# Three shared accumulator banks for the long convolutions in place of two and one

## The chip, the cores and the metric

The kernel runs on one core of a Trainium2 chip. The metric is the device time of one execution in microseconds (us), as the median of several runs. The core's engines work side by side and meet through semaphores: TensorE (PE in the profile; PEld is its loading of weights), VectorE (DVE), ScalarE (ACT), GpSimd (POOL) and SyncE (SP), which issues most of the DMAs. Matmuls write to accumulator banks; VectorE and ScalarE carry the results out of them into the core's working memory.

## The reference, cut to what matters

The kernel computes one encoder layer with two parallel mixers for a sequence of 1024 tokens and one of 512, width 1024. The part at hand is the gated long convolution, twice in a row over 512 channels:

```python
def hyena_mix(x1, x2, v, kspec, bias):
    def long_conv(z, ks, d):
        zf = jnp.fft.rfft(z, n=2 * L, axis=1)
        return jnp.fft.irfft(zf * ks[None], n=2 * L, axis=1)[:, :L] + d * z
    z = x1 * long_conv(v, kspec[:, 0], bias[0])
    return x2 * long_conv(z, kspec[:, 1], bias[1])
...
x = x + jnp.concatenate([y_hy, y_ml], axis=-1) @ w_out
```

`y_ml` is the other mixer, a chunked linear attention with 4 heads, run forwards and backwards. It is computed in the same stage of the kernel, in between the steps of the convolutions.

## The kernel before

The kernel is written by hand in stages, each a block that begins when all engines have left the one before: input projections with filters and gates, then the convolutions and heads (752 to 1152 us of the profile's span), then output projection and MLP. The change touches the middle stage alone, the function `long_convolutions_and_heads`.

The Fourier transforms are done as matmuls. The work is cut into four streams (st): 0 and 1 are the two channel halves of the long sequence (8 blocks of 128 tokens), 2 and 3 those of the short one (4 blocks). Each stream goes through two convolutions (o = 0, 1), in the order of `turns` (line 1397). For one stream and one convolution the steps are:

- **split** (TensorE line 1798, one for each block b): the outer part of the transform. ScalarE copies the bank out (line 1901), and SyncE spreads the result over the classes with a DMA (line 1655).
- **forward** (line 1810) and **inverse** (line 1821), for one pair of classes g: forward writes `xacc`, VectorE multiplies it with the filter's spectrum in three instructions (lines 1982 to 1984) into `prod`, inverse takes `prod` back, and ScalarE copies the bank out (line 1906). Inverse runs two pairs behind forward, so that TensorE's order is inverse(g-2), forward(g), inverse(g-1), forward(g+1), and so on.
- **join** (line 1832, one for each block), after DMAs (line 1661) have brought the classes back: VectorE multiplies the bank with the gate into `z` and so sets it free (line 1992).
- after a join of the first convolution, the **split** of the second one for the same block, two joins behind; after a join of the second one, the **turn** (line 1840): two transposes of `z` that ScalarE copies out with two instructions (line 1915).

A list `schedule`, written out in advance (lines 1422 to 1520), sets the order of all steps, and each engine runs its own part of the list in that order. The steps of the heads (keys, link, attend, turn_head and the norms) are spread into it by weights. They have three banks of their own (a, b, c). Around the middle of the stage little of the heads' work stands between the convolution's steps in some places and much in others.

Each of the eight banks holds 512 numbers per partition. Two belong to `xacc`, one to `gacc` (the inverses), two to `vyacc` (splits, joins and turns, in rotation), three to the heads. `before` (lines 1524 to 1542) holds, for each split, join and turn, the release of the step that used the bank last: `vy[-2]`, the last but one in the common list. An inverse waits for the copy of the inverse before it:

```python
if g:
    pe.wait_ge(sem["g_copied"], g)
```

All eight banks are in use before as well as after. TensorE takes its waits in order: whatever stands behind a waiting matmul waits too.

Of the kernel before, what the change touches and what calls it, by code (L numbers as in the profile page):

```python
# [17 lines left out]
ACT = mybir.ActivationFunctionType  # L18

P = 128  # L20
# [267 lines left out]
HC = HY // 2  # L288
# [1100 lines left out]
def long_convolutions_and_heads(nc, k_d, qk_d, tok_d, o_d, neg_max_d, ident, y_d, ahead, w_out):  # L1389
# [119 lines left out]
    schedule, credit, spent, at = [], 0.0, 0.0, 0  # L1509
# [12 lines left out]
    v_at, y_at, t_at, vy = {}, {}, {}, []  # L1522
    uses = {"a": [], "b": [], "c": []}
    before = {}
# [4 lines left out]
    for step in schedule:  # L1529
        kind, args = step[0], step[1:]  # L1530
        if kind == "split":
            v_at[args] = len(v_at)
            before[args] = vy[-2] if len(vy) >= 2 else None
            vy.append(("v_copied", len(v_at)))
        elif kind == "join":
            y_at[args] = len(y_at)
            before["join", args] = vy[-2] if len(vy) >= 2 else None
            vy.append(("z_ready", len(y_at)))
        elif kind == "turn":
            t_at[args] = len(t_at)  # L1540
            before["turn", args] = vy[-2] if len(vy) >= 2 else None
            vy.append(("copied", len(t_at)))
        elif kind == "keys":
            n = quads_before[args[0]] + args[1]
            take("a", step, ("k_copied", n + 1))
            take("b", step, ("weighted", n + 1))
        elif kind == "link":
            take("bc"[args[1] % 2], step, ("stated", links_before[args[0]] + args[1] + 1))
        elif kind == "attend":
            n = tiles_before[args[0]] + args[1]  # L1550
            take("a", step, ("combined", DIRS * n + 1))
            take("c", step, ("combined", DIRS * n + 2))
        elif kind == "turn_head":
            take("b", step, ("scaled", quads_before[args[0]] + args[1] + 1))
    vy_of = {step: n % 2 for n, step in enumerate(x for x in schedule if x[0] in ("split", "join", "turn"))}
    aged_at = {x: n for n, x in enumerate((j, i, d) for j in range(len(jobs)) for i in range(nts[jobs[j][1]]) for d in range(DIRS)
                                          if carried(d, jobs[j][1], outwards(jobs[j][1])[i]))}

    with ExitStack() as ctx:
# [25 lines left out]
        def classes(st):  # L1585
            i, b0 = slot(st)
            return class_slot[i][:, 2 * b0:2 * (b0 + len(blocks(st))), :]
# [10 lines left out]
        ss, rs = p.sb("ss", [P, big]), p.sb("rs", [P, big])  # L1598
        eps = p.sb("eps", [P, 1])
        xacc = [p.ps(f"xacc{b}", [P, 2, HC]) for b in range(2)]  # L1600
        gacc = p.ps("gacc", [P, 2, HC])
        vyacc = [p.ps(f"vyacc{b}", [P, 2, HC]) for b in range(2)]
        bank = {x: p.ps(f"bank_{x}", [P, CH]) for x in "abc"}
        names = ("v_ready v_copied x_ready multiplied g_ready g_copied "
                 "y_ready z_ready transposed copied "
# [23 lines left out]
        with nc.Block() as block:  # L1629
# [154 lines left out]
            def _(pe):  # L1784
# [28 lines left out]
                def inverse(g):  # L1813
                    o, st, t = pairs[g]
                    s, _ = streams[st]
                    pe.wait_ge(sem["multiplied"], g + 1)
                    if g:
                        pe.wait_ge(sem["g_copied"], g)
                    for u in range(2):
                        for i in range(2):  # L1820
                            last = pe.matmul(gacc[:, u, :], tab[s][:, t, u, 1 + i, :], prod[g % 2][:, u, i, :],
                                             start=i == 0, stop=i == 1)
                    last.then_inc(sem["g_ready"], 1)

# [73 lines left out]
            def _(act):  # L1898
# [4 lines left out]
                def copy_classes(g):  # L1903
                    o, st, t = pairs[g]
                    act.wait_ge(sem["g_ready"], g + 1)
                    act.activation(classes(st)[:, 2 * t:2 * t + 2, :], gacc[:, :, :], ACT.Copy).then_inc(sem["g_copied"], 1)

                def turned(st):
                    return classes(st)[:, 0:len(blocks(st)), :].rearrange("p r c -> p (r c)").rearrange(
# [827 lines left out]
```

## Time and profile before

| | us |
|---|---|
| median of 3 runs | 2400.17 |
| lowest and highest run | 2398.79, 2403.77 |
| the profiled execution, its own time | 2402.85 |
| span of the profile | 2401.1 |
| stage of convolutions and heads | from 752 to 1152 of the span |

The profiled execution's time is 1.75 us above its span, and 2.68 us above the median. The page of the profile gives the busy time of each engine. The list of waits says who waited for whom on TensorE. The timeline gives instructions in order of time, with the idle time before them and what ended it.

### The profile page before, as it was taken

How to read it: one execution, taken by the hardware profiler on the slowest of the kernel's cores; microseconds unless marked ns; L12 is line 12 of the kernel's file. 1: busy time of each engine (PE TensorE's matmuls, PEld its weight loads, DVE VectorE, ACT ScalarE, POOL GpSimd, SP SyncE). 2: the span in 40 equal slices, each digit the busy share in tenths (PEclk: the TensorE clock that was granted, in tenths of full speed). 3: DMA queues.
4: the chain of work that ended last, by engine and by line, in shares of the span. 5: the costliest groups of instructions: out<-in, count | busy, mean ns of one | idle time of the engine just before them, and what ended most of it. 6: DMA issues, size and time to landing. Idle time of an engine off the chain costs nothing.

```text
span 2401.1 us, 26125 instructions
## 1 busy us (share of the span) xinstructions
PE 2275.6 (95%) x10340; PEld 1859.8 (77%) x10340; DVE 1188.1 (49%) x1655; ACT 785.5 (33%) x1193; POOL 145.8 (6%) x163
## 2 busy tenths in 40 slices
PE   6999999998998979877899999999999999999998
PEld 4778877887786767666688888888888887888886
DVE  6676676554832756656456333343333334324332
ACT  5432333245434434534344211221222122324221
POOL 0221122000111000100000000000000000000000
PEclk9999999999999999999999999999999999999999
DMA  4344444454655665856645111121111112535442
GB/s 142 110 140 132 121 130 145 130 168 134 190 174 166 201 192 151 244 154 184 212 132 176 49 62 53 62 79 53 57 53 62 62 53 90 180 116 173 155 149 84
DMA packets 213588, 307.23 MB, mean 128 GB/s; under 512 B 15480, under 2 KB 143864, under 8 KB 213466
## 3 DMA queue, kind: packets, MB, share of 16 engines
q1 hardware_dynamic: 200858, 256.00, 35.0%
q0 software_dynamic: 11312, 46.14, 5.3%
q10 hardware_dynamic: 1296, 3.41, 0.4%
q8 instruction: 83, 1.36, 0.2%
q14 instruction: 39, 0.32, 0.0%
HBM read 207.38 MB, written 72.16 MB: 116 GB/s over the span
## 4 chain that ended last, share of the span: by engine, by line
PE 51%; DVE 0%; ACT 0%; issue 0%; DVEq 0%; POOL 0%
PE mlp_acc L128 10%; PE mlp_acc L130 10%; PE mlp_acc L129 10%; PE mlp_dacc L128 7%; PE mlp_dacc L129 7%; PE mlp_dacc L130 7%; PE mlp_acc L2596 0%; DVE out_s_lo L2494 0%; DVE up_u L245 0%; ACT up_u L2437 0%; DVE mlp_h_lo L2516 0%; DVE out_w_lo L2489 0%; DVE down_d_lo L2538 0%; ACT out_s_hi L2412 0%; DVE up_u L249 0%
## 5 line engine op out<-in xcount | busy, mean ns | idle before, releaser
L128 PE MATMUL mlp_acc<-mlp_h_hi,up_w_hi 128*128 128x512 f32 x1056 | 411.1, 389 | 0.2 <-DVE mlp_h_lo L2516 0.2
L130 PE MATMUL mlp_acc<-mlp_h_hi,up_w_lo 128*128 128x512 f32 x1056 | 410.8, 389 | 0.0
L129 PE MATMUL mlp_acc<-mlp_h_lo,up_w_hi 128*128 128x512 f32 x1056 | 410.8, 389 | 0.0
L2521 DVE TENSOR_TENSOR up_w_lo<-up_w_raw,up_w_hi 128x1024 fp32r<-128x1024 f32 x44 | 53.8, 1225 | 388.2 <-ACT up_w_hi L2429 388.2
L128 PEld LDWEIGHTS mlp_acc<-mlp_h_hi,up_w_hi 128*128 128x128 f32 x1056 | 198.2, 188 | 41.6 <-DVE mlp_h_lo L2516 0.6
L130 PEld LDWEIGHTS mlp_acc<-mlp_h_hi,up_w_lo 128*128 128x128 f32 x1056 | 198.2, 188 | 41.2
L129 PEld LDWEIGHTS mlp_acc<-mlp_h_lo,up_w_hi 128*128 128x128 f32 x1056 | 198.2, 188 | 41.1
L128 PE MATMUL mlp_dacc<-down_d_hi,down_s_hi 128*128 128x512 f32 x528 | 206.8, 392 | 5.3 <-DVE down_d_lo L2538 5.3
L129 PE MATMUL mlp_dacc<-down_d_lo,down_s_hi 128*128 128x512 f32 x528 | 206.6, 391 | 0.0
L130 PE MATMUL mlp_dacc<-down_d_hi,down_s_lo 128*128 128x512 f32 x528 | 206.4, 391 | 0.0
L2429 ACT ACTIVATE up_w_hi<-up_w_raw 128x1024 fp32r<-128x1024 f32 x44 | 46.6, 1059 | 460.1 <-PE mlp_acc L130 460.1
L128 PE MATMUL in_acc<-in_h_hi,in_w_hi 128*128 128x512 f32 x464 | 192.9, 416 | 2.0 <-DVE in_h_lo L1167 2.0
L130 PE MATMUL in_acc<-in_h_hi,in_w_lo 128*128 128x512 f32 x464 | 182.1, 392 | 0.0
L129 PE MATMUL in_acc<-in_h_lo,in_w_hi 128*128 128x512 f32 x464 | 181.5, 391 | 0.0
L2466 ACT ACTIVATE down_s_hi<-down_s_raw 128x1024 fp32r<-128x1024 f32 (+1 forms) x72 | 70.1, 986 | 220.8 <-DMA down_s_raw<-g_scratch 144.1
L1052 ACT ACTIVATE in_w_hi<-in_w_raw 128x1024 fp32r<-128x1024 f32 x58 | 61.4, 1059 | 212.9 <-PE in_acc L130 212.9
L2544 DVE TENSOR_TENSOR down_s_lo<-down_s_raw,down_s_hi 128x1024 fp32r<-128x1024 f32 (+1 forms) x72 | 79.8, 1132 | 93.6 <-ACT down_s_hi L2466 93.6
L128 PEld LDWEIGHTS mlp_dacc<-down_d_hi,down_s_hi 128*128 128x128 f32 x528 | 99.8, 189 | 26.6 <-DVE down_d_lo L2538 5.7
L129 PEld LDWEIGHTS mlp_dacc<-down_d_lo,down_s_hi 128*128 128x128 f32 x528 | 99.8, 189 | 20.9
L130 PEld LDWEIGHTS mlp_dacc<-down_d_hi,down_s_lo 128*128 128x128 f32 x528 | 99.8, 189 | 20.7
L1173 DVE TENSOR_TENSOR in_w_lo<-in_w_raw,in_w_hi 128x1024 fp32r<-128x1024 f32 x58 | 70.9, 1224 | 74.6 <-ACT in_w_hi L1052 74.5
L128 PEld LDWEIGHTS in_acc<-in_h_hi,in_w_hi 128*128 128x128 f32 x464 | 87.5, 189 | 24.9 <-issue 6.5
(243 smaller groups left out, 3902.2 us busy)
## 6 DMA issues: line engine op xcount, KB each, us to landing
in_w_raw<-arg_w_in_t SPq DMA_DIRECT2D x58, 512.0 KB, 3.6
down_s_raw<-g_scratch SPq DMA_DIRECT2D x48, 512.0 KB, 4.4
up_w_raw<-arg_w_up_t SPq DMA_DIRECT2D x44, 512.0 KB, 3.5
g_scratch<-up_prod POOLq DMA_DIRECT2D x22, 768.0 KB, 3.5
filt_tab<-arg_fwd SPq DMA_DIRECT2D x32, 512.0 KB, 3.8
mix_classes<-mix_split SPq DMA_DIRECT2D x48, 256.0 KB, 8.5
mix_kf<-k_scratch SPq DMA_DIRECT2D x48, 256.0 KB, 2.8
mix_split<-mix_classes SPq DMA_DIRECT2D x48, 256.0 KB, 5.0
```

What stands on the lines that cost most here:

```text
L128: pe.matmul(out, w_hi, x_hi, start=first, stop=False)
L129: pe.matmul(out, w_hi, x_lo, start=False, stop=False)
L130: return pe.matmul(out, w_lo, x_hi, start=False, stop=last)
L1052: act.activation(w_hi[b][:, :, :], raw[b][:, :, :], ACT.Copy).then_inc(sem["w_high"], 1)
L1173: dve.tensor_tensor(w_lo[b][:, :, :], raw[b][:, :, :], w_hi[b][:, :, :].bitcast(F32), ALU.subtract).then_inc(sem["w_low"], 1)
L2429: act.activation(w_hi[i % 2][:, :, :], raw[i % 2][:, :, :], ACT.Copy).then_inc(sem["w_high"], 1)
L2466: act.activation(s_hi[b][:, kts.start:kts.stop, :], s_raw[b][:, 0:len(kts), :], ACT.Copy).then_inc(s_high[b], 1)
L2521: dve.tensor_tensor(w_lo[i % 2][:, :, :], raw[i % 2][:, :, :], w_hi[i % 2][:, :, :].bitcast(F32), ALU.subtract).then_inc(sem["w_low"], 1)
L2544: dve.tensor_tensor(s_lo[b][:, ks, :], s_raw[b][:, 0:len(kts), :], s_hi[b][:, ks, :].bitcast(F32), ALU.subtract).then_inc(s_low[b], 1)
```

## The change

Splits, joins, turns and inverses share one ring of three banks. The release for which a step waits is now that of the third last user of the ring, `vy[-3]`, whatever its kind. Inverses are entered in the list and get a number in the ring. `gacc` is gone and `vyacc` has three buffers, so the stage still holds eight banks. No instruction is added, removed or moved on any engine; only the bank that a matmul writes and the semaphore for which it waits differ.

```diff
         if kind == "split":
             v_at[args] = len(v_at)
-            before[args] = vy[-2] if len(vy) >= 2 else None
+            before[args] = vy[-3] if len(vy) >= 3 else None
             vy.append(("v_copied", len(v_at)))
         elif kind == "join":
             y_at[args] = len(y_at)
-            before["join", args] = vy[-2] if len(vy) >= 2 else None
+            before["join", args] = vy[-3] if len(vy) >= 3 else None
             vy.append(("z_ready", len(y_at)))
         elif kind == "turn":
             t_at[args] = len(t_at)
-            before["turn", args] = vy[-2] if len(vy) >= 2 else None
+            before["turn", args] = vy[-3] if len(vy) >= 3 else None
             vy.append(("copied", len(t_at)))
+        elif kind == "inverse":
+            before["inverse", args] = vy[-3] if len(vy) >= 3 else None
+            vy.append(("g_copied", args[0] + 1))
...
-    vy_of = {step: n % 2 for n, step in enumerate(x for x in schedule if x[0] in ("split", "join", "turn"))}
+    vy_of = {step: n % 3 for n, step in enumerate(x for x in schedule if x[0] in ("split", "join", "turn", "inverse"))}
...
-        gacc = p.ps("gacc", [P, 2, HC])
-        vyacc = [p.ps(f"vyacc{b}", [P, 2, HC]) for b in range(2)]
+        vyacc = [p.ps(f"vyacc{b}", [P, 2, HC]) for b in range(3)]
...
                     pe.wait_ge(sem["multiplied"], g + 1)
-                    if g:
-                        pe.wait_ge(sem["g_copied"], g)
+                    free(before["inverse", (g,)])
+                    out = vyacc[vy_of["inverse", g]]
                     for u in range(2):
                         for i in range(2):
-                            last = pe.matmul(gacc[:, u, :], tab[s][:, t, u, 1 + i, :], prod[g % 2][:, u, i, :],
+                            last = pe.matmul(out[:, u, :], tab[s][:, t, u, 1 + i, :], prod[g % 2][:, u, i, :],
                                              start=i == 0, stop=i == 1)
...
-                    act.activation(classes(st)[:, 2 * t:2 * t + 2, :], gacc[:, :, :], ACT.Copy).then_inc(sem["g_copied"], 1)
+                    act.activation(classes(st)[:, 2 * t:2 * t + 2, :], vyacc[vy_of["inverse", g]][:, :, :], ACT.Copy).then_inc(sem["g_copied"], 1)
```

What a step waits for can be read from the program. TensorE in the last group of joins and turns of the stage (second convolution of stream 1), before: from the fourth join on, each waits for `z_ready` of the join directly before it, which VectorE sets when it has taken that join (only a turn lies between them). Repeated second matmuls are left out; the names are output bank, then stationary and moving operand.

```order
L1832 MATMUL mix_vyacc0<-mix_split0,mix_otab0 128x256 [waits mix_z_ready]
...
L1840 MATMUL mix_vyacc1<-all_ident,mix_z0 128x128 [waits mix_z_ready]
...
L1832 MATMUL mix_vyacc0<-mix_split0,mix_otab0 128x256 [waits mix_z_ready]
...
L1840 MATMUL mix_vyacc1<-all_ident,mix_z0 128x128 [waits mix_copied,mix_z_ready]
...
L1832 MATMUL mix_vyacc0<-mix_split0,mix_otab0 128x256 [waits mix_z_ready]
```

The same place after the change (line numbers are two higher): the third join waits for the copy of an inverse, the next one for the join two before it, and those after that for the copy of the turn two before (`copied`, ScalarE).

```order
L1834 MATMUL mix_vyacc1<-mix_split0,mix_otab0 128x256 [waits mix_g_copied]
...
L1842 MATMUL mix_vyacc2<-all_ident,mix_z0 128x128 [waits mix_z_ready]
...
L1834 MATMUL mix_vyacc0<-mix_split0,mix_otab0 128x256 [waits mix_z_ready]
...
L1842 MATMUL mix_vyacc1<-all_ident,mix_z0 128x128 [waits mix_z_ready]
...
L1834 MATMUL mix_vyacc2<-mix_split0,mix_otab0 128x256 [waits mix_copied]
```

The order of the instructions is the same in both; the banks go round by three, and a join no longer waits for the join directly before it.

## Rows read from the trace of the kernel before

**Rows 1.** The page, part 1: busy us, share of span, instructions.

```profile
PE 2275.6 (95%) x10340; PEld 1859.8 (77%) x10340; DVE 1188.1 (49%) x1655; ACT 785.5 (33%) x1193; POOL 145.8 (6%) x163
```

**Rows 2.** Waits on TensorE, 752 to 1152: waiter <- releaser: total us, times, longest.

```profile
PE mix_vyacc L1832 <- DMA mix_split<-mix_classes: 17.9, 3, 9.5
PE mix_vyacc L1832 <- DVE mix_z L1992: 8.2, 13, 1.2
...
PE mix_gacc L1821 <- DVE mix_prod L1984: 4.9, 5, 2.8
...
PE mix_vyacc L1798 <- ACT mix_split L1901: 4.5, 3, 2.1
...
PE mix_vyacc L1840 <- ACT mix_classes L1915: 1.1, 2, 0.6
...
PE mix_gacc L1821 <- ACT mix_classes L1906: 0.9, 2, 0.5
```

**Rows 3.** Timeline, last joins and turns: start us, duration, engine, instruction [idle <- releaser].

```profile
1140.21 1.13 PE L1832 MATMUL mix_vyacc<-mix_split,mix_otab 128*128 128x256 f32 x4 [0.97 <-DVE mix_z L1992]
...
1141.86 1.13 PE L1832 MATMUL mix_vyacc<-mix_split,mix_otab 128*128 128x256 f32 x4 [0.30 <-DVE mix_z L1992]
1142.83 0.38 PE L1840 MATMUL mix_vyacc<-all_ident,mix_z 128*128 128x128 f32 x2
1143.03 0.42 DVE L1992 TENSOR_TENSOR mix_z<-mix_vyacc,mix_gate 128x256 f32<-128x256 f32 x1
1143.24 0.63 ACT L1915 ACTIVATE mix_classes<-mix_vyacc 128x128 f32<-128x128 f32 x2 [1.02 <-PE mix_vyacc L1840]
...
1143.51 1.13 PE L1832 MATMUL mix_vyacc<-mix_split,mix_otab 128*128 128x256 f32 x4 [0.30 <-DVE mix_z L1992]
```

**Rows 4.** Timeline: a turn, a join and what follows, without a wait.

```profile
950.77 0.38 PE L1840 MATMUL mix_vyacc<-all_ident,mix_z 128*128 128x128 f32 x2
950.99 1.03 PE L1832 MATMUL mix_vyacc<-mix_split,mix_otab 128*128 128x256 f32 x4
...
1073.24 1.03 PE L1832 MATMUL mix_vyacc<-mix_split,mix_otab 128*128 128x256 f32 x4
1074.11 0.60 PE L1890 MATMUL mix_bank_b<-all_ident,mix_state 128*128 128x128 f32 x4
```

**Rows 5.** Timeline, start of the joins of stream 3, first convolution.

```profile
901.26 1.89 PE L1832 MATMUL mix_vyacc<-mix_split,mix_otab 128*128 128x256 f32 x8
...
903.64 0.76 DVE L1992 TENSOR_TENSOR mix_z<-mix_vyacc,mix_gate 128x256 f32<-128x256 f32 x2
...
904.12 1.13 PE L1832 MATMUL mix_vyacc<-mix_split,mix_otab 128*128 128x256 f32 x4 [0.97 <-DVE mix_z L1992]
```

**Rows 6.** Timeline, splits of stream 1, first convolution.

```profile
975.38 1.28 ACT L1935 ACT_TABLE_LOAD   x1
...
977.99 1.10 PE L1798 MATMUL mix_vyacc<-mix_z,mix_otab 128*128 128x256 f32 x4 [1.39 <-ACT mix_split L1901]
```

**Rows 7.** Timeline, joins and splits of stream 1, after the first convolution.

```profile
1067.59 1.10 PE L1798 MATMUL mix_vyacc<-mix_z,mix_otab 128*128 128x256 f32 x4 [2.14 <-ACT mix_split L1901]
...
1070.63 1.91 PE L1832 MATMUL mix_vyacc<-mix_split,mix_otab 128*128 128x256 f32 x4
```

**Rows 8.** Timeline, inverses and forwards with no heads between (PEld: weight loads).

```profile
853.33 1.59 PEld L1821 LDWEIGHTS mix_gacc<-mix_prod,mix_tab 128*128 128x128 f32 x8 [0.29 <-issue]
...
855.36 0.60 ACT L1906 ACTIVATE mix_classes<-mix_gacc 128x512 f32<-128x512 f32 x1 [1.57 <-PE mix_gacc L1821]
...
856.07 1.59 PEld L1821 LDWEIGHTS mix_gacc<-mix_prod,mix_tab 128*128 128x128 f32 x8 [0.29 <-issue]
...
859.07 1.59 PEld L1821 LDWEIGHTS mix_gacc<-mix_prod,mix_tab 128*128 128x128 f32 x8 [0.54 <-DVE mix_prod L1984]
```

**Rows 9.** Windows: stretch, us, busy PE PEld DVE ACT POOL (instructions), PEclk, DMA share, GB/s.

```profile
790.00:792.00 2.00, 1.54 (x10) 1.14 (x9) 1.16 (x3) 0.80 (x2) 0.00 (x0) 1.00 1.10 351
...
992.00:994.00 2.00, 2.00 (x13) 1.79 (x12) 0.29 (x1) 0.43 (x2) 0.00 (x0) 1.00 0.15 58
```

## The prediction

> **What bounds the kernel now.** First the page: TensorE is busy for 95% of the span, VectorE for half of it [rows 1]. So a gain has to come out of TensorE's idle time, some 125 us in all. The change can reach only the part between 752 and 1152 us. There I read the list of TensorE's waits by who ended them [rows 2]. The longest, 17.9 us in three waits, are joins that wait for the DMAs that bring the classes back. That is data and not a bank, and the change doesn't touch it. What was ended by the release of a bank is smaller: joins that waited for VectorE to take an earlier join (8.2 us in 13 waits), splits that waited for ScalarE's copy (4.5 us in 3), turns that waited for a copy (1.1 us in 2), inverses that waited for one (0.9 us in 2). Together that is 14.7 us, 0.6% of the time. All else in the timeline is there to answer two questions: what a wait costs beyond the idle time shown, and what is late next once it is gone.
>
> **Joins (8.2 us).** In the last group of the stage, joins and turns alternate with little between them. From one join to the next it takes 1143.51 - 1141.86 = 1.65 us [rows 3]. Without a wait a turn is followed after 0.22 us and a join after 0.87 us [rows 4], so 1.09 us would do. The stop costs 0.56 us, where its row shows 0.30: after a stop the overlap with the next weight load is lost as well. If each of the 13 stops hides another 0.26 us, they cost 8.2 + 3.4 = 11.6 us. That is the upper bound. After the change a join waits for the third last user of the ring. In this group that is the turn before last: its copy takes 0.63 us on ScalarE [rows 3] and has a join and a turn, 1.09 us, to be done in, so the wait goes, but narrowly. What is late next is VectorE: the turn needs `z` of its own block. At the start of the groups the third join waited, because VectorE was still busy with the multiplications of the last forward and took the first two joins only at 903.64, in 0.76 us; the third started at 904.12 after 0.97 us [rows 5]. With three banks it goes first, and the split or turn behind it waits until the first join is taken, at about the time at which the join started before. TensorE has then done 0.87 us of work more by that point: nearly the whole wait, not more. Lower bound: about half, 4 us, if in most places the split or turn waits for its data as long as the join did. I take the 8.2 us of the row: the hidden 3.4 us stand against the turns and splits that now wait for data.
>
> **Splits (4.5 us).** Eight splits in a row, stream 1: two waits, because ScalarE loads an activation table (1.28 us) and does exponentials between its copies; the second wait is 1.39 us [rows 6]. The third is 2.14 us at 1067.59 [rows 7]. One bank more lets TensorE run one split further ahead. At 1067.59 that covers the whole wait, since the release for which the split would wait is then that of a join on VectorE. In the row of eight I keep 1.7 of 2.4 us, because ScalarE still has all the copies to do and behind them the scaling of the keys. Sum 3.8, bounds 2 and 4.5 us. What could be late next is the first forward of stream 1 (after 994 us), which needs the DMAs of these splits. They run at full load, but their share is down to 0.15 from 992 us on [rows 9]: some 2 us of slack, enough for the 1.7.
>
> **Inverses (0.9 us and small stops).** Where pairs follow each other with no heads between, the copy of one inverse ends at 855.36 + 0.60 = 855.96, and the weights of the next are loaded from 856.07 on, after a gap of 0.29 us [rows 8]: each inverse waits for the copy of the one before, and the pair takes 856.07 - 853.33 = 2.74 us. With three banks this wait is gone for good. But the next row shows who comes then: the inverse at 859.07 was ended by VectorE's multiplication, 3.00 us after the one before it. VectorE needs three instructions for each pair, and the norms of the heads besides. In these stretches a faster TensorE only waits longer for VectorE (the 4.9 us of [rows 2] grow). I take 0.3 us; bounds 0 and 2 us (0.9 and some seven gaps like this one, of which 2.74 - 12 x 0.216 = 0.15 us can be had; 0.216 us is a quarter of the 0.87 us of a join's four matmuls).
>
> **Leading splits.** The 16 splits at the start stop the same way, six times, 6 x 0.15 = 0.9 us in all. After them the DMAs run at full load until 792 us (share 1.10 [rows 9]), with loads issued at the start of the stage, which come no earlier now, and VectorE's multiplications need filter spectra that queue behind them. I take 0, bounds 0 and 0.9.
>
> **The clock.** Some 3 us after the idle 2.14 us a join takes 1.91 us in place of 1.03 [rows 4, 7]: 1.2 GHz instead of 2.4. The eight matmuls of the keys before it were slowed likewise, by about as much. That is 1.7 us that goes if the idle time before it was its cause. I take 0.7. The Trainium skill (TensorE: Matmul & The Clock Gate, A second HAM failure mode: psum-queue depth-cycling) says that a kernel that cycles through its accumulator banks in each iteration idles so often for a moment that the clock falls back again and again. By that rule more cycling could cost clock. The trace agrees only with the direction from idle time to clock, and the change shortens idle times, so by it the 1.7 us would come back whole, and the sum would be 14.0.
>
> **What the change could cost.** An inverse after a group of splits or turns now waits for ScalarE's copy of the third last of them, and no longer only for the copy of an inverse that is long done. There are six such places. A turn group ends with turns of 0.22 us, so a wait that stood at the last turn (the 1.1 us) partly moves to the inverse. Since the 1.1 us aren't in my sum I take nothing off; the bounds are a gain of 1.1 and a loss of 2 us.
>
> **Sum.** 8.2 + 3.8 + 0.3 + 0 + 0.7 = 13.0 us. The stage ends with a barrier, and the next one starts with weights and rows that are long loaded, so its 13 us come through whole: 2402.85 - 13.0 = 2389.9 for the profiled execution, which lies 2.7 us above the median. From the median: 2400.17 - 13.0 = 2387.2 us.
>
> **The rivals.**
> A: the waits change their name. Joins, turns and splits need data from the same VectorE and ScalarE whose release they waited for, both engines take their work in order, and these now set the pace. For it: [rows 8] and the third join in [rows 5], behind which the split has to wait anyway. Against it: VectorE is busy only half of the time, and in [rows 3] 0.42 us per join. It would leave half of the joins and the split at 1067.59: 4.1 + 2.1 = 6 us at most, 2394 to 2398, say 2396.
> B: the DMAs decide. The three long waits [rows 2] end when the last transfer lands, and if these queues are full on their own account, everything gained ahead of them is lost there. For it: the full load up to 792 us [rows 9]. Against it: the transfers are issued by progress of the splits and inverses, so they move along. Only what lies behind the last of the three, the last group (about 3 us), and the splits would then count: 2395. The Trainium skill (TensorE: Matmul & The Clock Gate, HAM oscillation — how this bites in real kernels) tells of a kernel with waits for DMAs in which double buffering of the accumulators brought nothing further; by that the time would stay at 2400.
> C, slower: the common ring ties the inverses to ScalarE. In each of the six places the inverse waits for a copy behind a table load and exponentials, 1.39 us as at 977.99 [rows 6], and six times that is 8.3 us: 2400 + 8.3 less what the joins of the last group still save (3) = 2405. It decides only if ScalarE is more than two steps of TensorE (1.7 us) behind at the end of the groups.
> D: all bounds are reached: 11.6 + 4.5 + 2 + 0.9 + 1.7 = 20.7 us, 2379.5; nearer to it than to my sum, with the turns' 1.1: 2382.
>
> **How the numbers follow.** My forecast (2385 to 2391) 0.57; A 0.16; B 0.09; C 0.04; D 0.14. The range 2381 to 2395.5 takes in the forecast, most of D and part of A and B, and leaves out about 2 in 10. A measurement of this kernel can tell 0.2% (4.8 us, so 2395.4) from no change. Faster: forecast, D, half of A and of B: 0.84. Within 0.2%: 0.12. Slower: 0.04.
>
> **What the profile will show.** Right: the joins' waits for VectorE fall from 8.2 us to under 2, and the period in the last group from 1.65 to about 1.1 to 1.2 us; the wait at 1067.59 is gone, and the join behind it takes 1.03 us; the end of the stage comes some 13 us earlier; the waits for DMAs stay near 17.9 us; those of inverses for VectorE's multiplications grow above 4.9. Wrong: turns and splits wait for VectorE for as long as the joins did (A); the waits for DMAs grow by the gain (B); inverses wait for copies of turns or splits (C).

## The result

The changed kernel takes 2391.55 us (median of 7 runs, 2386.75 to 2393.61); the kernel before, run beside it, 2402.01 us (2396.91 to 2407.64, 7 runs). The ratio is 0.9949, with a 95% interval of 0.9935 to 0.9962: 12.3 us faster by the ratio, 10.5 by the medians. A second comparison of the same two kernels gave 2390.61 us and 0.9946 (0.9934 to 0.9959). 2387.2 us were predicted, with a range of 2381 to 2395.5.

Two lines have been added ahead of all that follows, so L1832 of before is L1834 here (joins), L1798 is L1800 (splits), L1840 is L1842 (turns), L1821 is L1823 (inverses), L1810 is L1812 (forwards); all but the forwards now write to `mix_vyacc`.

The busy time of the engines is as in [rows 1]; TensorE's is 7.4 us less, 4.7 of it inside the stage of convolutions and heads:

```profile
PE 2268.2 (95%) x10340; PEld 1861.4 (78%) x10340; DVE 1189.0 (50%) x1655; ACT 785.2 (33%) x1193; POOL 145.8 (6%) x163
```

TensorE's waits between 752 and 1152 us, the answer to [rows 2] (waiter <- releaser: us in total, times, longest):

```profile
PE mix_vyacc L1834 <- DMA mix_split<-mix_classes: 17.0, 3, 8.5
...
PE mix_vyacc L1823 <- DVE mix_prod L1986: 7.2, 8, 2.9
...
PE mix_bank_b L1892 <- DVE mix_e L2007: 2.7, 3, 1.4
PE mix_xacc L1812 <- issue: 2.0, 2, 1.8
PE mix_vyacc L1800 <- ACT mix_split L1903: 1.5, 1, 1.5
...
PE mix_vyacc L1834 <- ACT mix_classes L1917: 0.7, 1, 0.7
PE mix_vyacc L1842 <- DVE mix_z L1994: 0.7, 3, 0.3
...
PE mix_vyacc L1823 <- ACT mix_classes L1917: 0.4, 1, 0.4
```

The 8.2 us in which joins waited for VectorE's take of an earlier join are gone to the last one. Splits wait 1.5 us for a copy in place of 4.5. New are 0.7 us of a join that waits for a turn's copy, and 2.0 us before forwards (L1812), of which the kernel before shows nothing. The inverses' waits for VectorE's multiplications have grown from 4.9 to 7.2 us, and one wait of the heads for VectorE (L1892; L1890 before) from 1.1 to 2.7 us.

The last group of the stage, which answers [rows 3] (timeline of TensorE alone: start, duration, instruction, idle before it and its releaser):

```profile
1130.91 0.41 PE L1842 MATMUL mix_vyacc<-all_ident,mix_z 128*128 128x128 f32 x2 [0.32 <-DVE mix_z L1994]
1131.15 1.03 PE L1834 MATMUL mix_vyacc<-mix_split,mix_otab 128*128 128x256 f32 x4
1132.02 0.38 PE L1842 MATMUL mix_vyacc<-all_ident,mix_z 128*128 128x128 f32 x2
1132.24 1.03 PE L1834 MATMUL mix_vyacc<-mix_split,mix_otab 128*128 128x256 f32 x4
...
1135.26 1.13 PE L1834 MATMUL mix_vyacc<-mix_split,mix_otab 128*128 128x256 f32 x4 [0.69 <-ACT mix_classes L1917]
```

From one join to the next it takes 1132.24 - 1131.15 = 1.09 us, where [rows 3] had 1.65. The turns are not late: VectorE needs 0.42 us for a join, and the turn that reads it stands a whole join later. Only the last join stops, and ScalarE's own timeline says why. A table load stands ahead of the copies, and that is the one new dependence that costs something:

```profile
1132.44 0.64 ACT L1917 ACTIVATE mix_classes<-mix_vyacc 128x128 f32<-128x128 f32 x2 [0.44 <-PE mix_vyacc L1842]
1133.09 1.28 ACT L1969 ACT_TABLE_LOAD   x1
1134.39 0.30 ACT L1969 ACTIVATE mix_rs<-mix_ss,mix_eps 128x8 f32<-128x8 f32 x1
1134.60 1.08 ACT L1917 ACTIVATE mix_classes<-mix_vyacc 128x128 f32<-128x128 f32 x4
```

**How far one profile can be trusted.** The stage's own length can be read from two rows of a timeline: its first split and the first matmul of the stage behind it. Before:

```profile
753.14 17.57 PE L1798 MATMUL mix_vyacc<-mix_z,mix_otab 128*128 128x256 f32 x64 [4.52 <-PEq L119]
...
1158.89 0.76 PE L128 MATMUL mlp_dacc<-out_w_hi,out_s_hi 128*128 128x512 f32 x1 [7.95 <-DVE out_w_lo L2489]
```

After:

```profile
752.15 15.74 PE L1800 MATMUL mix_vyacc<-mix_z,mix_otab 128*128 128x256 f32 x64 [4.52 <-PEq L119]
...
1146.80 0.76 PE L128 MATMUL mlp_dacc<-out_w_hi,out_s_hi 128*128 128x512 f32 x1 [7.90 <-DVE out_w_lo L2491]
```

That is 405.75 and 394.65 us, 11.1 less. Of these, 4.7 us are busy time of TensorE (330.5 before, 325.9 now, for the same 1712 matmuls) and 6.4 idle time. What follows the stage is as long as before (1242.2 and 1241.8 us to the end of the span), so the gain does come through whole. But the profile of the changed kernel's second measurement has 751.39 to 1149.99, 398.60 us, 7.2 less. Two executions of one kernel differ by 4 us inside this stage, so the size of an effect is taken below from the medians and ratios of many runs, and the profile says where it arises.

### The profile page after: what moved, and what is told of

The parts are those of the page before. It is cut to its first block, busy times and chain, and to the rows that moved or that the text cites. A ratio compares the mean times of both kernels' runs of the same rounds, so it can differ in the third digit from the quotient of the medians.

```text
span 2388.6 us, 26125 instructions
## 1 busy us (share of the span) xinstructions
PE 2268.2 (95%) x10340; PEld 1861.4 (78%) x10340; DVE 1189.0 (50%) x1655; ACT 785.2 (33%) x1193; POOL 145.8 (6%) x163
## 4 chain that ended last, share of the span: by engine, by line
PE 51%; DVE 0%; ACT 0%; issue 0%; DVEq 0%; POOL 0%
PE mlp_acc L128 10%; PE mlp_acc L129 10%; PE mlp_acc L130 10%; PE mlp_dacc L128 7%; PE mlp_dacc L130 7%; PE mlp_dacc L129 7%; PE mlp_acc L2598 0%; DVE out_s_lo L2496 0%; DVE up_u L245 0%; ACT up_u L2439 0%; DVE mlp_h_lo L2518 0%; DVE out_w_lo L2491 0%; DVE down_d_lo L2540 0%; ACT out_s_hi L2414 0%; DVE up_u L249 0%
```

## Experiments

All were timed in five rounds beside the kernel before, which was at 2403.3 to 2403.9 us each time. "Stage" is the length read as above, of one execution. Each of the experiments 1 to 11 is the changed kernel with the edit shown. An interval of 0.0012 to each side is 3 us.

| | kernel | median us | ratio to before (95%) | stage us |
|---|---|---|---|---|
| 0 | the changed kernel again | 2390.61 | 0.9946 (0.9934 to 0.9959) | 398.60 |
| 1 | shared ring, but two banks | 2404.14 | 1.0009 (1.0001 to 1.0018) | 405.95 |
| 2 | inverses wait as before | 2389.27 | 0.9945 (0.9933 to 0.9958) | 391.70 |
| 3 | joins wait as before | 2399.97 | 0.9986 (0.9976 to 0.9996) | 405.73 |
| 4 | splits and turns wait as before | 2396.17 | 0.9970 (0.9958 to 0.9981) | 399.17 |
| 5 | heads moved to the forward of stream 1 | 2393.61 | 0.9957 (0.9941 to 0.9973) | 395.74 |
| 6 | one ring of five, forwards too | 2391.15 | 0.9949 (0.9932 to 0.9965) | 394.33 |
| 7 | 5 and 6 together | 2386.58 | 0.9933 (0.9916 to 0.9950) | 389.87 |
| 8 | only splits wait as before | 2396.77 | 0.9970 (0.9958 to 0.9982) | 402.90 |
| 9 | heads moved to the first joins | 2397.61 | 0.9978 (0.9969 to 0.9987) | 403.38 |
| 10 | 6 and 9 together | 2394.62 | 0.9962 (0.9949 to 0.9975) | 398.88 |
| 11 | 7 again | 2389.36 | 0.9945 (0.9928 to 0.9962) | 390.75 |

**0. The same kernel once more.**

> The changed kernel once more, as the yardstick for the kernels beside it. Expected 9 to 13 us below the kernel before, as in its first timing (2402.0 to 2391.6 us); in the trace the last group's period from join to join near 1.1 us, and a forward of stream 1 that waits some 2 us for its DMAs near 990 us.

It repeats the first result, and gives the stage's spread told of above.

**1. Is it the third bank, or the sharing?** The change does two things: it puts the inverses in the ring, and it gives the ring a third bank. Here only the first is kept.

```diff
-            before[args] = vy[-3] if len(vy) >= 3 else None
+            before[args] = vy[-2] if len(vy) >= 2 else None
...
-    vy_of = {step: n % 3 for n, step in enumerate(...)}
+    vy_of = {step: n % 2 for n, step in enumerate(...)}
...
-        vyacc = [p.ps(f"vyacc{b}", [P, 2, HC]) for b in range(3)]
+        vyacc = [p.ps(f"vyacc{b}", [P, 2, HC]) for b in range(2)]
```

> One shared ring as in the changed kernel, but of two banks (each step waits for the last but one user, inverses too). Theory 'third bank': what pays is that a join, split or turn waits for the third last user in place of the second last; so the joins' waits for VectorE come back (8 us, 13 waits), splits wait 4 to 5 us, and the time is within 2 us of the kernel before. Rival 'inverses': the gain comes from inverses no longer waiting for the copy of the inverse directly before; they don't here either, so half of the gain or more (6 us and up) would remain.

2404.14 us, 0.1% slower than before, and its waits on TensorE are those of [rows 2]:

```profile
PE mix_vyacc L1834 <- DVE mix_z L1994: 7.9, 13, 1.2
...
PE mix_vyacc L1800 <- ACT mix_split L1903: 4.5, 3, 2.1
```

So the sharing brings nothing, and costs some 2 us by the ratio (0.2 to 4.3): splits, joins, turns and inverses get by with two banks in all nearly as well as with the three of before (two, and one for inverses alone). The inverses' own bank was hardly needed, and the whole gain is that of a third bank for the others.

**2. The inverses' share.** The inverse waits again for the copy of the one before it, beside its place in the ring.

```diff
                     free(before["inverse", (g,)])
+                    if g:
+                        pe.wait_ge(sem["g_copied"], g)
```

> The changed kernel with one wait added: each inverse also waits for the copy of the inverse before it, as in the kernel before. Theory 'third bank': VectorE's multiplications are next in line anyway, so no more than 1 us is lost (within 1 us of the changed kernel). Rival 'inverses': 5 us or more are lost.

2389.27 us, 0.9945 against 0.9946. The inverses' own release brings nothing that could be measured. The changed kernel's timeline shows the reason, and answers [rows 8]:

```profile
852.14 1.70 PEld L1823 LDWEIGHTS mix_vyacc<-mix_prod,mix_tab 128*128 128x128 f32 x8
...
854.76 1.67 PEld L1823 LDWEIGHTS mix_vyacc<-mix_prod,mix_tab 128*128 128x128 f32 x8
...
858.14 1.59 PEld L1823 LDWEIGHTS mix_vyacc<-mix_prod,mix_tab 128*128 128x128 f32 x8 [0.85 <-DVE mix_prod L1986]
```

The gap of 0.29 us has gone and the pair takes 2.62 us in place of 2.74. The next inverse then waits 0.85 us for VectorE in place of 0.54: the tenths saved are waited out one pair later.

**3. The joins' share.** Splits, turns and inverses keep the three banks; a join also waits for the release of the second last split, join or turn, as before the change.

```diff
+            old["join", args] = own[-2] if len(own) >= 2 else None
...
                     free(before["join", (o, st, b)])
+                    free(old["join", (o, st, b)])
```

> The changed kernel with one wait added: each join also waits for the release of the last but one split, join or turn, as in the kernel before (13 waits, 8.2 us). Theory 'third bank': 6 to 9 us are lost, so the time is 1 to 5 us above... below the kernel before by 3 to 5 us, the part of the splits. Rival 'inverses': under 2 us are lost. Rival 'splits': the joins' waits only move to the splits and turns behind them, so 2 to 3 us are lost.

2399.97 us: 0.9986 against 0.9946, so 0.4% or some 9.5 us of the gain are lost, just above the 6 to 9 expected. The old wait stands where it stood, and the forward of stream 1 shows a longer wait than in the changed kernel:

```profile
PE mix_vyacc L1841 <- DVE mix_z L2001: 8.2, 13, 1.3
...
PE mix_xacc L1818 <- issue: 3.5, 1, 3.5
```

**4. The share of splits and turns.** The same edit at the splits and the turns in place of the joins.

```diff
                     free(before[o, st, b])
+                    free(old[o, st, b])
...
                     free(before["turn", (st, b)])
+                    free(old["turn", (st, b)])
```

> The changed kernel, with its three banks, in which splits and turns (not joins, not inverses) also wait for the release of the second last split, join or turn before them, as they did before the change. It holds the splits' share. Theory (joins carry the gain, of the splits' 4.5 us the forward of stream 1 lets through only 2, since it then waits for its DMAs): 2 to 4 us slower than the changed kernel, and the wait of that forward for its DMAs at 990 us is gone. Rival (the splits' gain comes through whole): 5 to 6 us slower. Rival (splits bring nothing): within 1 us of the changed kernel.

2396.17 us, 0.9970: 5.7 us of gain lost by the ratios, 5 by the medians. That is above what I had expected for it (2 to 4) and at the edge of the rival by which the splits' gain comes through whole. The forward's wait is down to 0.2 us, as expected.

**8. Splits alone.** The edit at L1800 only, to see whether the turns, which the prediction had counted at nothing, hold part of these 5 us.

> The changed kernel in which only the splits also wait for the release of the second last split, join or turn; turns, joins and inverses are as in the changed kernel. It takes the turns out of the loss of 3.6 us (profile) to 5 us (medians) that splits and turns gave together. Theory (the turns' release cost about what their rows grew by, 1 to 2 us, which the prediction counted at nothing): 2 to 3.5 us slower than the changed kernel. Rival (turns cost nothing, as predicted): 4 to 5 us slower, as with the turns held back too.

2396.77 us, again 0.9970. So nothing shows that the turns hold anything, which speaks for the prediction's nothing, though two intervals of 3 us to each side can't exclude the 1 to 2 us of my theory. The splits' waits are back, and even longer than the 4.5 us of before:

```profile
PE mix_vyacc L1807 <- ACT mix_split L1910: 6.0, 3, 2.4
```

The whole difference lies in the first wait of stream 1's splits, 2.44 us where it was 0.94 before:

```profile
969.19 3.88 PE L1807 MATMUL mix_vyacc<-mix_z,mix_otab 128*128 128x256 f32 x16 [2.86 <-DMA mix_z<-tok_scratch]
975.51 1.10 PE L1807 MATMUL mix_vyacc<-mix_z,mix_otab 128*128 128x256 f32 x4 [2.44 <-ACT mix_split L1910]
```

In the profile of before the same 16 matmuls took 5.41 us, since the granted clock was 0.50 from 971 to 973 us (here 1.00). The split behind them starts 6.35 us after the first one there and 6.32 here: it goes by ScalarE's copy, and the 1.5 us of slow matmuls only filled a part of the wait for it. So the 4.5 us that the list of before showed for the splits would have been 6.0 at full clock.

This run also bears on the clock in another place. It has the idle time of [rows 7] again, almost to the hundredth, but what comes behind it is not slowed:

```profile
1067.03 1.10 PE L1807 MATMUL mix_vyacc<-mix_z,mix_otab 128*128 128x256 f32 x4 [2.13 <-ACT mix_split L1910]
...
1069.30 1.03 PE L1841 MATMUL mix_vyacc<-mix_split,mix_otab 128*128 128x256 f32 x4
```

The granted clock is 1.00 here, 2.4 GHz. In [rows 7] the join at the same place took 1.91 us, with 0.52.

**Where the splits' gain goes.** The timeline of the changed kernel from the splits of stream 1 to its first forward, and the DMAs at its end (windows: stretch, us, busy time of each engine, clock, DMA share, GB/s):

```profile
965.87 4.58 PE L1800 MATMUL mix_vyacc<-mix_z,mix_otab 128*128 128x256 f32 x20 [3.11 <-DMA mix_z<-tok_scratch]
971.93 1.10 PE L1800 MATMUL mix_vyacc<-mix_z,mix_otab 128*128 128x256 f32 x4 [1.48 <-ACT mix_split L1903]
...
974.42 1.96 PE L1800 MATMUL mix_vyacc<-mix_z,mix_otab 128*128 128x256 f32 x8
...
990.58 1.10 PE L1812 MATMUL mix_xacc<-mix_classes,mix_tab 128*128 128x256 f32 x4 [1.78 <-issue]
```

```profile
986.00:988.00 2.00, 2.00 (x13) 1.79 (x12) 0.36 (x2) 0.37 (x1) 0.00 (x0) 1.00 1.03 298
988.00:990.00 2.00, 0.80 (x7) 0.61 (x5) 0.49 (x2) 1.20 (x4) 0.00 (x0) 1.00 0.55 164
990.00:992.00 2.00, 1.42 (x7) 1.30 (x8) 0.23 (x1) 1.04 (x4) 0.00 (x0) 1.00 0.11 45
```

The same places in the kernel before:

```profile
969.16 5.41 PE L1798 MATMUL mix_vyacc<-mix_z,mix_otab 128*128 128x256 f32 x16 [2.59 <-DMA mix_z<-tok_scratch]
...
980.26 1.89 PE L1798 MATMUL mix_vyacc<-mix_z,mix_otab 128*128 128x256 f32 x8
...
994.41 1.03 PE L1810 MATMUL mix_xacc<-mix_classes,mix_tab 128*128 128x256 f32 x4
```

From the first split to the last two it took 980.26 - 969.16 = 11.10 us, and takes 8.55 now: 2.55 us won. From the first split to the forward it took 25.25 us and takes 24.71: 0.54 are left. Nearly all of the other 2 us is the forward's wait (1.78). The profile names no releaser for it ("issue"), but the code has the forward wait there for the DMAs that bring the splits to `classes`, and it begins when the DMA share, at 1.03 until 988 us, drops. The DMAs were at full load before the change too, and don't get faster. The wait is there in each profile of a kernel with three banks for all its splits and this order, with another size each time: 1.78 us here, 2.78 in run 0, 0.42 in run 2, 3.47 in run 3. In run 0 the forward starts at 994.84 us, 26.19 after the first split at 968.65; in run 3 it is 992.05 - 965.79 = 26.26 us. There nothing of the splits' gain is left at all. With two banks for the splits the forward doesn't wait, or 0.2 us at most, and starts 25.25 us (before), 25.33 (run 1), 25.55 (run 4) and 26.72 (run 8) after the first split.

**5. Can the cover be moved there?** TensorE has other work, the heads, whose place in the order can be moved. A gap in the list puts a stretch of it at one place; its size is in the units in which a forward counts 0.9 and an inverse 1.8, so that a unit is about 1 us of TensorE. Two such units are taken from ahead of the joins at 1048 us and put behind the splits of stream 1.

```diff
     split_all(0, 1)
-    conv.append(("gap", 5))
+    conv.append(("gap", 7))
...
-    conv.append(("gap", 9))
+    conv.append(("gap", 7))
     join_all(0, 1)
```

> The changed kernel with the gaps in the order of work shifted: 7 in place of 5 gap units of heads' work stand behind the splits of stream 1 (ahead of its first forward), and 7 in place of 9 ahead of its joins at 1048 us. The sum is the same. If the 1.9 us at the forward of stream 1 (it waits for the DMAs that bring the splits) are a lack of cover, they go. Theory: the wait at 990 us goes, and 0 to 2 us of it arrive at the end. Rival: the join at 1048 us, which waits 5.9 us for its DMAs, now has less ahead of it, waits longer by the same 1.9 us, and the time is that of the changed kernel.

The rival fits better: 2393.61 us, if anything slower, though the intervals overlap. The wait before forwards falls to 0.4 us in all, and the join at 1048 us, which waited 5.91 us in the changed kernel, has this row instead (timeline, TensorE):

```profile
1051.87 4.94 PE L1834 MATMUL mix_vyacc<-mix_split,mix_otab 128*128 128x256 f32 x12 [9.02 <-DMA mix_split<-mix_classes]
```

It has grown by 3.1 us, where the forwards' waits lost 1.6.

**9. The same at the longest wait.** Six units of heads' work go ahead of the first joins, where TensorE idles 8.5 us; they are drawn evenly from the rest of the stage.

```diff
             if turn_at.get(turn) == g:
+                if turn == (0, 0):
+                    conv.append(("gap", 6))
                 join_all(*turn)
```

> The changed kernel with a gap of 6 units of heads' work put ahead of the first joins (at 870 us), where TensorE waits 8.5 us for the DMAs that bring the classes back. The work is drawn evenly from all the rest of the stage. Theory (every stretch is short of the same heads' work, so cover only moves): the wait at 870 us falls to 1 to 3 us, the waits for DMAs at 990, 1048 and 1125 us grow, and 0 to 2 us of 6 arrive. Rival (in the stretches of pairs TensorE sets the pace, so heads taken from there shorten them): 4 to 7 us faster than the changed kernel, 2384 to 2387 us.

2397.61 us: more than half of the change's gain is lost (0.9978 against 0.9946). Both expectations are missed: the theory allowed 0 to 2 us faster, the rival 4 to 7, and it is 7 us slower. The waits on TensorE:

```profile
PE mix_vyacc L1836 <- DMA mix_split<-mix_classes: 11.6, 2, 7.4
PE mix_xacc L1814 <- issue: 9.6, 2, 6.3
PE mix_vyacc L1802 <- DMA mix_z<-tok_scratch: 7.7, 1, 7.7
```

The 8.5 us before the joins are gone. In their place the forward just ahead of them waits 6.3 us, and the splits of stream 1 wait 7.7 us for their input where they waited 3.1. These three sum to 28.9 us; in the changed kernel the same three were 17.0 + 2.0 + 3.1 = 22.1, so the 7 us lie in them. The window from 862 to 870 us (columns as above), first in the changed kernel,

```profile
862.00:870.00 8.00, 0.05 (x1) 0.05 (x1) 0.73 (x1) 0.65 (x1) 2.71 (x2) 0.71 0.99 337
```

then in run 9:

```profile
862.00:870.00 8.00, 6.86 (x38) 5.80 (x36) 7.80 (x9) 7.18 (x16) 4.67 (x2) 1.00 1.09 248
```

The DMAs are at full load in both. TensorE, idle in the one and busy in the other, waits for them in the end, whatever instruction it then stands at. That explains why the idle time came back; why 7 us more of it came than had gone is open.

**6, 7, 10 and 11. More banks.** The forwards join the ring, which then has all five banks, each step waiting for the release of the fifth last.

```diff
+        elif kind == "forward":
+            before["forward", args] = vy[-5] if len(vy) >= 5 else None
+            vy.append(("multiplied", args[0] + 1))
...
-    vy_of = {step: n % 3 ...
+    vy_of = {step: n % 5 ...
...
-        xacc = [p.ps(f"xacc{b}", [P, 2, HC]) for b in range(2)]
-        vyacc = [p.ps(f"vyacc{b}", [P, 2, HC]) for b in range(3)]
+        vyacc = [p.ps(f"vyacc{b}", [P, 2, HC]) for b in range(5)]
```

> The changed kernel with forwards in the ring too: splits, forwards, inverses, joins and turns share one ring of five banks (three and the forwards' two), each waiting for the release of the fifth last. Theory (what bank waits are left, 1.5 us of splits for copies and about 1 us of joins and inverses, goes; all that waits for DMAs stays): 0 to 2 us faster than the changed kernel. Rival (a forward's bank is held until VectorE's multiplication, so the ring is now tied to it in the pairs): 1 to 5 us slower.

2391.15 us, the time of three banks. The splits' and joins' waits for copies are gone from the list of waits. But the forward waits again, the longer of two such waits being 1.5 us:

```profile
PE mix_vyacc L1813 <- issue: 2.5, 2, 1.5
```

That is the lower edge of the theory (0 to 2 us). Nothing in the waits speaks for the rival, that the pairs suffer: the inverses wait 6.5 us for VectorE's multiplications, where it was 7.2. But the interval, 4 us to each side, doesn't exclude the lower end of the 1 to 5 us that it named.

> The ring of five with the shifted gaps, both at once. Theory: the two are independent: the sum of what each brought alone, 0 to 4 us faster than the changed kernel. Rival: with the splits still earlier, the forward of stream 1 waits for its DMAs in spite of the shifted gaps, and the time is that of the better of the two.

Run 7 (ring of five, and the gaps of run 5) was the fastest of all, 2386.58 us, at the upper end of the theory's 0 to 4 us, though neither part alone was faster than three banks. So it was run again:

> The ring of five with 7 gap units behind the splits of stream 1 and 7 ahead of the joins at 1048 us, a second time on its own, since its time, 2386.58 us, was the lowest of all, while each of its two parts alone was no faster than the three banks (2391.15 and 2393.61). If it is a better kernel the ratio to the kernel before is again 0.992 to 0.9945, some 4 us below the three banks. If it was chance, the ratio is 0.9945 to 0.996, as that of the three banks and of the ring of five alone.

2389.36 us, 0.9945: on the border of the two expectations. Both of its stages, 389.87 and 390.75 us, are shorter than the two of the changed kernel, but so is that of run 2 (391.70). It is at least as fast as the changed kernel, perhaps by 2 to 3 us; this is not settled.

> The ring of five with the same gap of 6 units ahead of the first joins. Theory (the ring of five brought nothing alone in the medians, 2391.15 against 2391): the time is that of the three banks with this gap, within 2 us. Rival: with more banks the ring adds 2 to 4 us of gain once a DMA wait no longer swallows it, as the ring of five with the other shifted gaps, 2386.58, seemed to show.

Run 10 was 3 us below run 9 (2394.62 against 2397.61, intervals that overlap), 1 us outside what the theory allowed. It points the same way as run 7: with the order of work changed, five banks seem worth 3 to 6 us more than three (runs 7, 11 and 10 against 5, 5 and 9, by the ratios), which the intervals don't settle. It is no better than the changed kernel.

## Why the prediction was right, and where it was off

**The whole.** 13.0 us were predicted; 12.3 were measured by the ratio, 10.5 by the medians. Of the 4.4 us between 2387.2 and 2391.55 us, 1.8 are the base: the kernel before was at 2402.01 us in this comparison and at 2400.17 in the runs that the sum started from. The source was the third bank, as the sum had it: run 1, with sharing alone, has none of the gain. That the total came so close is in part luck. In the two profiles the stops for a bank fall by 12.1 us (from 14.7 to 1.5 + 0.7 + 0.4), but the idle time of the stage by 6.4 only: the waits for multiplications, those before forwards and one of the heads took 2.3 + 2.0 + 1.6 us back, of which the prediction named the first without a price and held the second to be covered by slack. In return TensorE's busy time in the stage fell by 4.7 us, of which the sum had the 0.7 for the clock and, set against new waits, the 3.4 hidden behind the joins' stops. The joins' busy time didn't fall (53.3 and 54.4 us), but the splits' went from 51.7 to 47.7 us, in part because fewer of them fell into a stretch of half clock.

**Joins, 8.2 us (bounds 4 and 11.6).** Right. Holding the joins back costs 9.5 us (run 3), and with the splits held back the rest of the change brings 7.2 us (run 8, 0.9970). The mark set for it, waits under 2 us and a period of 1.1 to 1.2, came out as none and 1.09. Rival A, that turns and splits wait instead, has little in its favour: they wait 0.7 + 0.2 us for VectorE, where the turns alone had 0.8 before, against 8.2 gone.

**Splits, 3.8 us.** The size is right within what the runs can tell. Without the splits 5.7 us are missing (run 8 against run 0), and with splits but not joins the kernel is 3.4 us faster than before (run 3, 0.9986). The difference between the two is no more than their intervals allow. The step that failed is the last one of that part, "some 2 us of slack, enough for the 1.7". The splits won more than 1.7, 2.55 us (the row that priced them was short by 1.5 us, as run 8 shows), and the slack was not there. I had read it from the DMA share of one profile, which fell at 992 us, and had taken the landing to move along with the splits. But the DMAs work there on a full queue of their own: with the splits earlier, the forward got its data 24.1 to 26.3 us after the first split (the changed kernel and runs 0, 2 and 3; in run 2 it is 991.18 - 967.04), where it stood at 25.25 us before. So, against that profile, the slack was 1.1 us at best, and of this row of splits 0 to 1.1 us arrive, not 1.7. With the 2.1 us of the third wait that makes 2.1 to 3.2 us. Run 8 puts the splits at 5.7 us, with an interval that reaches down to about 1.5. A part of what goes beyond the 3.2 shows in its own profile, where the forward starts 26.72 us after the first split, up to 2.6 us later than with three banks; four of the splits' matmuls ran at half clock there (2.04 us in place of 1.10). Whether that belongs to two banks or to that one execution is open. The third wait went whole, as predicted; there the changed kernel has

```profile
1058.55 1.03 PE L1800 MATMUL mix_vyacc<-mix_z,mix_otab 128*128 128x256 f32 x4
...
1060.91 1.13 PE L1834 MATMUL mix_vyacc<-mix_split,mix_otab 128*128 128x256 f32 x4
```

in place of [rows 7]: no idle time ahead of the split, and the join at full clock. (A wait of 0.2 us ahead of the join's weights, for ScalarE, is what is late next.)

**Inverses, 0.3 us.** Run 2 measures the inverses' own wait at 0, within some 4 us; the account of it, that VectorE takes the gain back, is in the rows of experiment 2. VectorE works there without a pause, 3.38 us for each pair (its multiplications begin at 853.53 and 856.92 us before, at 852.61 and 855.99 now).

**Leading splits, 0.** The 64 matmuls of the leading splits take 15.74 us where they took 17.57, 1.8 us less. Half of that is the six stops: ScalarE's last 13 copies span 10.36 us in place of 11.28, 0.92 less, and the term had 0.9. The rest is a shorter stretch of half clock at their start. Nearly none of it lasts: an inverse later waits for VectorE where it waited for nothing before,

```profile
796.84 1.99 PE L1823 MATMUL mix_vyacc<-mix_prod,mix_tab 128*128 128x256 f32 x8 [1.38 <-DVE mix_prod L1986]
```

and 2.83 us in run 0. Right for the reason given: VectorE's multiplication ahead of that inverse waited 2.22 us for the DMA of its filter spectrum (L1984, 3.67 in run 0), where it was 0.56 before.

**Turns to inverses, 0.** Right: an inverse waits for a turn's copy once, 0.4 us, where the turns' own waits of 1.1 us and the inverses' of 0.9 went. Rival C had the mechanism that does occur once, a table load on ScalarE ahead of the copies that free a bank. But it met a join of the last group, and cost 0.69 us.

**DMA waits.** 17.0 us against 17.9, near the forecast. Rival B, that the DMAs take back what is gained ahead of them, is right in one place of the four, the forward of stream 1. At the joins it doesn't hold: the one that started at 1055.51 us, after a wait of 5.92, starts at 1048.38 now, after 5.91, so its transfers moved along with the work that issues them. Beside it stood the Trainium skill's remark (TensorE: Matmul & The Clock Gate, HAM oscillation — how this bites in real kernels) that double-buffered accumulators gave no further gain in a kernel that had been reordered so that it waits for DMAs less often. The two times that the page gives for it, 126.6 and 125.5 us, are 0.9% apart, so it can't decide on a gain of this size. Here 0.5% came, beside three long waits for data that stayed, and runs 3 and 8 put it down to the stops for a bank.

**The clock, 0.7 us.** This term can't be confirmed. The slow join at 1070 us is gone, but run 8 has the same idle time with a fast join behind it, so idle time there doesn't decide alone, and the argument that tied 1.7 us to it fails. The changed kernel has a slow stretch of its own elsewhere, at the start of the last group:

```profile
1125.23 4.28 PE L1834 MATMUL mix_vyacc<-mix_split,mix_otab 128*128 128x256 f32 x12 [2.58 <-DMA mix_split<-mix_classes]
```

and in run 0, the same kernel, the same twelve matmuls are fast:

```profile
1129.39 2.86 PE L1834 MATMUL mix_vyacc<-mix_split,mix_otab 128*128 128x256 f32 x12 [2.62 <-DMA mix_split<-mix_classes]
```

Run 0 is slow at the forward of stream 1 instead (2.05 us for four matmuls). These three profiles have a few such stretches of 1.2 GHz behind an idle time, not always the same ones, and the mean granted clock is 0.982 before and after (0.980 in run 0). The Trainium skill's rule on cycling through accumulator banks (TensorE: Matmul & The Clock Gate, A second HAM failure mode: psum-queue depth-cycling) would have let more cycling cost clock; no run here shows that it did.

## What to carry to other kernels

Read the stops for a bank from the list of waits, by their releaser: here thirteen of them, 8.2 us in all, came back nearly at the price shown when a third bank was added, and the bank could be had from a step (the inverse) that hardly needed one of its own. Slack ahead of a wait for a DMA is not what one profile's DMA share seems to leave: if the queue is full on its own account, the landing doesn't move with the step that issues it, and the gain ahead of it is lost. Moving filler work to where TensorE idles for such a transfer didn't help either (runs 5 and 9): the idle time came back at the next transfer, and in run 9 with 7 us more. And a wait in a profile can be too short: where the matmuls ahead of it ran at half clock, they had filled a part of it (0.94 us shown, 2.44 at full clock).

## What the hardware showed unexpectedly

Two executions of the same kernel differ by 4 us within one stage of 395 us, a third of the effect under study, while its total times lie 8 us apart at most (2385.96 to 2394.12 us, the 13 runs of the changed kernel). It isn't the clock: TensorE is busy for 325.9 us of the stage in both, and the 4 us are idle time, spread over waits that differ a little each (before forwards 2.0 and 3.6 us, for multiplications 7.2 and 7.9, for the joins' DMAs 17.0 and 17.4). The stretches of half clock change their place all the same: twelve matmuls behind the same wait of 2.6 us took 4.28 us in one execution (granted clock 0.50 from 1126 to 1128 us) and 2.86 in the other, the one whose stage is longer. A stretch at 1.2 GHz in a single profile should not be counted as a cost that a change can remove, unless a second profile has it at the same place.
